# A trunk step with gathered experts on one core: expert sums assigned by the mixing item behind them, and layer 1's modulation made by PE alone

## What is computed

```python
def trunk_layer(x, cond, p, lambda_init, cache):
    sh1, sc1, g1, sh2, sc2, g2 = jnp.split(jax.nn.silu(cond) @ p['w_mod'] + p['b_mod'], 6, axis=-1)
    mix, ctx_tensors = token_mixing(modulate(x, sh1, sc1), p, lambda_init, cache)
    x = layer_norm_affine(DEEPNORM_ALPHA * x + g1[:, None] * mix, p['ln1_g'], p['ln1_b'])
    ffn = peer_ffn(modulate(x, sh2, sc2), p['peer_w_q'], p['peer_subkeys'], p['peer_u'], p['peer_v'])
    x = layer_norm_affine(DEEPNORM_ALPHA * x + g2[:, None] * ffn, p['ln2_g'], p['ln2_b'])
...
    def expert_block(args):
        xt, e, g = args
        act = jax.nn.gelu(jnp.einsum('td,tkd->tk', xt, jnp.take(u_tab, e, axis=0)), approximate=False) * g
        return jnp.einsum('tk,tkd->td', act, jnp.take(v_tab, e, axis=0))
```

## Time and the profile before

| | before |
|---|---|
| time, median of 3 runs | 3299.2 us (3292.91 to 3309.16) |
| time of the profiled execution | 3296.41 us |
| its span | 3294.6 us |
| mean granted TensorE clock | 0.888 |
| bytes moved | 1071.02 MB, mean 325 GB/s |

### The profile page before, as it was taken

The page is one execution under the profiler, slowest core; times in us unless marked ns, Lnnn a source line. Parts: engine busy times, 40 slices in busy tenths (PEclk is TensorE's granted clock), DMA queues, the critical chain, the costliest instruction groups (busy, mean ns, idle before and its releaser), DMA issues.

```text
span 3294.6 us, 29983 instructions
## 1 busy us (share of the span) xinstructions
PE 2524.8 (77%) x8820; PEld 1448.2 (44%) x8820; DVE 2202.0 (67%) x5396; ACT 710.8 (22%) x1797; POOL 1713.7 (52%) x1540
## 2 busy tenths in 40 slices
PE   8897988989767787668885779697958666667666
PEld 3585635757453223346652234475736322222222
DVE  4534577675769976756659744868665978856665
ACT  1121123451112220033211111254111211111111
POOL 0000275453437775445557744554433688777775
PEclk9898998989889998889997989898979898799988
DMA  8856598878778999979999978887966899999998
GB/s 327 299 187 222 175 377 311 295 268 324 276 262 334 376 396 414 364 292 374 408 412 343 359 274 302 330 325 271 352 231 240 308 339 342 357 378 415 416 412 313
DMA packets 296223, 1071.02 MB, mean 325 GB/s; under 512 B 33536, under 2 KB 36352, under 8 KB 295296
## 3 DMA queue, kind: packets, MB, share of 16 engines
q0 software_dynamic: 221184, 805.40, 64.9%
q1 hardware_dynamic: 71712, 253.16, 20.8%
q10 hardware_dynamic: 3168, 10.55, 0.8%
HBM read 1065.67 MB, written 3.31 MB: 324 GB/s over the span
## 4 chain that ended last, share of the span: by engine, by line
PE 42%; DVE 22%; POOL 16%; issue 10%; DMA 8%; ACT 1%; DVEq 0%; ACTq 0%; SPq 0%; POOLq 0%
POOL ring L1669 10%; PE psum L707 9%; PE psum L797 9%; POOL work L1669 6%; PE psum L786 5%; PE psum L956 5%; DVE ring L1221 4%; DMA ring<-in_peer_v,experts 3%; DVE work L1319 3%; PE psum L822 3%; PE psum L938 2%; PE psum L748 2%; DMA wring<-in_wpack 2%; DMA ring<-in_peer_u,experts 2%; DVE work L1221 2%
## 5 line engine op out<-in xcount | busy, mean ns | idle before, releaser
L707 PE MATMUL psum<-ring,wdiag 128*128 128x512 f32 x1680 | 915.7, 686 | 383.3 <-DMA ring<-in_peer_v,experts 210.2
L1669 POOL DMA_INDIRECT ring<-in_peer_u,experts x488 | 562.4, 1153 | 989.3 <-DVE dots L1221 455.8
L1669 POOL DMA_INDIRECT ring<-in_peer_v,experts x620 | 675.0, 1089 | 404.3 <-PE psum L707 210.8
L707 PEld LDWEIGHTS psum<-ring,wdiag 128*128 128x128 f32 x1680 | 341.3, 216 | 888.2 <-issue 537.5
L1221 DVE CUSTOM_DVE_ANT_0 work<-work 128x1024 f32<-128x1024 f32 x280 | 338.5, 1225 | 129.5 <-DMA work<-in_peer_u,experts 127.8
L1669 POOL DMA_INDIRECT work<-in_peer_u,experts x280 | 313.9, 1121 | 96.6 <-issue 83.2
L1221 DVE CUSTOM_DVE_ANT_0 ring<-ring,h2a 128x1024 f32<-128x1024 f32 x256 | 305.1, 1222 | 73.2 <-DMA ring<-in_peer_u,experts 72.3
L1221 DVE CUSTOM_DVE_ANT_0 ring<-ring,work 128x1024 f32<-128x1024 f32 x232 | 280.1, 1223 | 101.2 <-DMA ring<-in_peer_u,experts 99.8
L990 ACT ACTIVATE acts<-dots 128x2 f32<-128x2 f32 x384 | 77.8, 203 | 1104.1 <-DVE dots L1221 1056.7
L797 PE MATMUL psum<-work,wring 128*128 128x256 f32 (+1 forms) x1696 | 311.6, 342 | 0.6 <-DVE work L1630 0.6
L797 PEld LDWEIGHTS psum<-work,wring 128*128 128x128 f32 x1696 | 275.6, 195 | 43.4 <-issue 15.4
(11 more groups left out here) (201 smaller groups left out, 2872.7 us busy)
## 6 DMA issues: line engine op xcount, KB each, us to landing
wring<-in_wpack SPq DMA_DIRECT2D x374, 512.0 KB, 6.9
ring<-in_wpack SPq DMA_DIRECT2D x94, 512.0 KB, 5.6
ring<-in_peer_v,experts POOLq DMA_INDIRECT x620, 6.4
ring<-in_peer_u,experts POOLq DMA_INDIRECT x488, 6.4
work<-in_peer_u,experts POOLq DMA_INDIRECT x280, 6.3
work<-in_rows ACTq DMA_DIRECT2D x4, 1024.0 KB, 8.4
work<-in_peer_v,experts POOLq DMA_INDIRECT x148, 6.3
work<-in_rpb ACTq DMA_DIRECT2D x2, 1024.0 KB, 13.1
```

The costliest lines, as they stand in the source:

```text
L707: last = nc.tensor.matmul(psum[:, 6 + q, :], wdiag[:, SUM_NO[e] % SMALL, :], row(V_SLOT[e])[:, 512 * q:512 * (q + 1)], start=(e % KSEL == ...
L1669: pool.indirect_dma_start(row(slot), None, a[table], index).then_inc(got[slot], 16)
```

## The change

Three things are edited.

- `SHARE` goes. For each expert, `vector_sums()` looks up the item of `WORK` that stands behind the step of its sum, and takes a fraction for VectorE by the item's kind: in latent stages from `LATENT_SHARE`, in context stages 1/4, and none where the item is `topk`, `norms` or `ln1`. The first eight experts of a tile go to PE. Where no item is left, the fraction is 1/4. VectorE's sums by tile: 53, 18, 39, 84, 18, 30 before, and 53, 14, 9, 63, 9, 30 now, 178 instead of 242.
- In layer 1 all twelve modulation parts are `mod` items, on PE; parts 4 to 9 were `macc` items. Layer 0 stays as it is.
- ScalarE evacuates layer 1's parts and their `modt` (parts 0 to 9 were VectorE's).

The cost table is unchanged, but a `mod` item counts 7 where two `macc` counted 12, so the steps are dealt a little differently over layer 1's context stage: 13 steps instead of 16 stand between its first projection and its norms.

```diff
-SHARE = [[(44, 2, 3), (112, 1, 2)], [(72, 1, 3)], [(8, 1, 2), (72, 1, 8)], [(8, 3, 4), (104, 1, 2)], [(56, 1, 4)], [(8, 1, 4)]]
-def by_vector(e):
-    k = e % KSEL
-    part = [(n, of) for first, n, of in SHARE[e // KSEL] if k >= first]
-    return bool(part) and (k + 1) * part[-1][0] // part[-1][1] > k * part[-1][0] // part[-1][1]
...
 def mod_by_vector(l, j):
-    return 4 <= j < (12 if l == 0 else 10)
+    return l == 0 and j >= 4
...
             out += ([modt(l, 3 + j)] if j else [])
+            if j < 6:
+                out += [("macc", m, 4 + j, k, l) for k in range(2)] if mod_by_vector(l, 4 + j) else [("mod", m, 4 + j, l)]
...
+LATENT_SHARE = {"proj": (1, 1), "mix": (1, 1), "pq": (1, 1), "gate": (2, 3), "br": (2, 3), "ps": (1, 1), "h2": (1, 1),
+                "s": (1, 3), "pt": (1, 3), "o": (1, 3), "ot": (1, 3), "tt": (1, 3), "kv": (1, 3), "mqt": (1, 3), "mkt": (1, 3)}
+def vector_sums():
+    at, out = schedule(), []
+    for e in range(ALL_EXPERTS):
+        k, place = e % KSEL, at[e // PAIR + LAG_SUM]
+        x = WORK[place] if place < len(WORK) else ("end", -1)
+        n, of = LATENT_SHARE.get(x[0], (0, 1)) if x[1] in LATENT else (0, 1) if x[0] in ("topk", "norms", "ln1") else (1, 4)
+        out.append(2 * LAG_SUM <= k and (k + 1) * n // of > k * n // of)
+    return out
...
     if kind in ("mod", "modt"):
-        return "v" if x[2] < 10 or mod_by_vector(x[3], x[2]) else "a"
+        return "a" if x[3] else "v"
...
-                    elif kind == "mod" and it[2] >= 10:
+                    elif kind == "mod" and EVAC_BY[INDEX[it]] == "a":
                         full(act, it)
-                        if it[3]:
-                            full(act, modt(it[3], 9))
+                        if it[2] > 1:
+                            full(act, modt(it[3], it[2] - 2))
+                        else:
+                            act.wait_ge(experts_ready, HEAD_GROUPS * TILE_NO[(l, 0)])
+                            act.wait_ge(cols_ready, DEPTH)
                         taken(nc.scalar.copy(v.modacc[0:2, it[2] % 2, :], bank(it)[0:2, :]))
```

More of the change, by code:

```diff
@@ L318, in schedule @@
             at[n] = last
-    assert at == sorted(at) and all(s[0][0] >= 2 * LAG_SUM for s in SHARE)
+    assert at == sorted(at)
     return at
@@ L341, with by_vector, sums_before @@
 PROGRAM = program()
+LATENT_SHARE = {"proj": (1, 1), "mix": (1, 1), "pq": (1, 1), "gate": (2, 3), "br": (2, 3), "ps": (1, 1), "h2": (1, 1),
[8 more added lines that the diff above has]
+    return out
+VECTOR_SUM = vector_sums()
+def by_vector(e):
+    return VECTOR_SUM[e]
+SUM_NO, _sums = [], {True: 0, False: 0}
+for _e in range(ALL_EXPERTS):
+    SUM_NO.append(_sums[by_vector(_e)])
+    _sums[by_vector(_e)] += 1
+def sums_before(e, vector):
+    return sum(by_vector(i) == vector for i in range(e))
 XN_NO, _made = {}, 0
@@ L756, in _ @@
                         else:
[L757 removed]
+                            pe.wait_ge(macc_ready, j - 3)
                         for n in range(4):
@@ L1496, in _ @@
                             normalised(m, i, i)
-                    elif kind == "mod" and it[2] < 10:
+                    elif kind == "mod" and EVAC_BY[INDEX[it]] == "v":
                         full(dve, it)
@@ L1500, in _ @@
                             full(dve, modt(it[3], it[2] - 2))
-                        elif it[3]:
-                            full(dve, modt(0, 11))
                         taken(nc.vector.tensor_copy(v.modacc[0:2, it[2] % 2, :], bank(it)[0:2, :]))
```

11 lines of the change are left out of this document (2 added, 9 removed).

## The result

The changed kernel takes 3207.22 us (median of 4 runs, 3187.23 to 3213.1) against 3296.05 us before in the same comparison: a ratio of 0.970, 95% interval 0.9663 to 0.9738, that is 86 to 111 us less (the medians lie 89 apart, the ratio over all runs gives 99). The forecast was 3266 with a range down to 3232: the direction was right, the size not.

What follows compares the result with a forecast made beforehand. No single engine was taken to bound the kernel, so stretches were priced separately: -12 +15 -10 -10 -16 = -33 from 3296.4, plus 2.8 to the median, gave 3266 us; range for 8 in 10: 3232 to 3304.

Steps and rivals of the forecast that it cites:

- A: Layer 1's modulation loop: without the VectorE link 140 us against 168, -28; three steps displaced elsewhere +16; net -12 us.
- the third rival: Faster by more: displaced steps fill the norms gap and POOL issues faster beside less VectorE work; 3238 us, chance 0.14.
- The limit of about 358 GB/s a core: HBM to SBUF limit: the new loop could not be under 161 us, making its term +9; 3 in 100.
- B: Rest of layer 1's context stage: 19 more sums on PE up to the first top-k piece, net +15 us.
- C: Context-stage top-k: 13 VectorE sums go, eight where VectorE is the bound, the others worth 0; -10 us.
- The heads of layer 1: Latent stage of layer 1: 14 more head sums on PE, 9 priced at 1.72 us, +15; bounds -6 and +24.
- The rival with 38 paid sums: Slower, PE becomes the bound: every PE sum added in heads and context stage is paid, +65; total 3313 us, chance 0.14.
- Layer 0's +8.6: Attention heads of layer 0's latent stage: 5 more sums on PE, costing 8.6 us.
- the queries with `ln1`: Latent stages: 7 fewer PE sums at the queries, -12 each layer; fewer VectorE sums in `ln1`, -5 and -6 us.
- the top-k starts' direction: Start of the latent top-k: 4 fewer VectorE sums in each layer, -5 us each.
- the norms of layer 1: Layer 1's latent stage: 4 fewer VectorE sums in the norms, partly on its chain, -3 us.
- Tile 4's -3: Nine fewer VectorE sums in tile 4, where POOL's gather issues are the chain; -3 us.

Runs made afterwards that it cites:

- the modulation alone: The changed kernel with the old table of sums (242 on VectorE), so only layer 1's modulation moves to PE: 3256.16 us, 0.9863 of the kernel before.
- the sums alone: The changed kernel with layer 1's parts 4 to 9 and their evacuations back on VectorE, so only sums move: 3238.29 us, 0.9794 of the kernel before.
- `relief`: The kernel before without 19 VectorE expert sums in layer 1's heads, which nobody makes: 3368.79 us, 0.9973 of the kernel before on the same chip.
- `evac_vector`: The changed kernel with layer 1's modulation parts evacuated by VectorE instead of ScalarE: 3298.4 us, 0.9748 of the kernel before on the same chip.
- `warm_loop`: The kernel before with eight zero products on PE before the weight wait in layer 1's later projections: 3391.46 us, 1.0002 of the kernel before.
- the fraction 0: The changed kernel with no VectorE sums beside attention-head items (fraction 0 for 1/3, 21 fewer): 3227.05 us, 0.976 of the kernel before.

## Why the prediction fell short

**A, the modulation loop: the link was right, the size and what follows from it were not.** The new loop "has no VectorE link", and PE's round was forecast at 19 us and takes 19.51. But I set the loop's length by the transfers, at 140 us. It took 125.5 in that cut, and its window of 131 us moved 131 * 0.414 = 54 MB, not 57.5: I had counted the bytes of a stretch of 168 us, of which a shorter one holds fewer gathers that merely pass by. The loop is bound by PE and by transfers at once (125.74 of 131 us busy, DMA share 1.03). It gave 43 instead of 28. The three displaced steps were to cost 16 elsewhere: they are worth 18.5 in the loop and putting them back changes no total, so as a price that term stands. Net of them the loop gives 25 where 12 stood. But the modulation alone gave 40, so the net -12 was short by 28, and some 15 of them are neither in the loop nor in the steps. The likely place is the norms gap. I had left it to the third rival; before, it moved 172 GB/s, and with the change 413 (34 and 32 us, so 5.8 and 13.2 MB). The modulation alone fills it as well, the sums alone do not:

```profile
1367.00:1401.00 34.00, 26.03 (x125) 16.41 (x123) 19.39 (x51) 11.00 (x30) 12.06 (x11) 0.90 1.03 413
```

```profile
1401.00:1435.00 34.00, 26.78 (x137) 18.06 (x135) 18.93 (x53) 10.10 (x24) 3.31 (x4) 0.90 0.54 191
```

7.4 MB more in a gap that got no longer are 18 us of transfers at 413 GB/s (an estimate), in a stage whose rest is full of transfers. That is the first half of the third rival's mechanism. The gap is filled with the 16 steps put back too (393 GB/s), so it goes with the faster loop and not with the displaced steps; that it is worth the 15 us is argued, since no run isolates it and the scatter is of that size. The limit of about 358 GB/s a core in the Trainium skill's "DMA: Bandwidth & Descriptors", section "Where 436 GB/s comes from", to which I gave 3 in 100, fell: 414 GB/s over these 131 us. The Trainium skill's section gets it by halving a stack's 716 GB/s between two cores, and here one core ran the kernel alone.

**B and C, the rest of the context stage.** "7 * 1.72 = +12" for the sums on PE's chain, +15 with the others: -0.2 in the change, and the sums alone cost 3.7 us there. Too large, likely by the same error as the heads. On the two other chips it is 5.7 and 8.2 us (from the last projection to the key scores 305.2 in `relief` against 310.9 in `evac_vector`, 305.5 in `warm_loop` against 313.7 in the change), so a part of the price is real. C: I let 8 of 13 VectorE sums count and called the other five hidden; the stretch gave 14.7 with the sums alone, 1.13 us for each of the 13, within a scatter of some us. In the change it gave 14.0 where C and the +16 of the steps made +6.

**The heads of layer 1, the term whose mechanism was wrong: +15, measured +0.8** (261.7 to 262.5 us up to the first output product; the row's -2.7 has the output products in it). By size it comes second, 14 us, behind the 28 of A's net. The step was "Where PE has the chain each costs 1.72; where VectorE has it nothing". Two things were missing. The price: 0.86 us, since PE was 88% busy and the granted clock rises from 0.89 to 0.95 with more work. And the other side: where VectorE has the chain, taking a sum from it gains, 0.74 measured, and I had written zero there, a cost without its credit. The two near-equal numbers make the whole move nearly free, up to the point where the fraction 0 shows the price again (+8 us). The rival with 38 paid sums fell by the same numbers. Layer 0's +8.6 is not shown wrong: its first output product begins at 816.9 us in the mean of the eight kernels with the new sums, 810.7 in that of the five with the old ones.

**Right:** the queries with `ln1` (-17 forecast, -13.2 measured; -18, -20.1 in layer 1), the top-k starts' direction (-5 forecast in layer 1, -7.9 measured), the evacuations at nothing, the last tile bound by its transfers, and POOL as what is late next in the top-k.

**Wrong in sign:** the norms of layer 1 (-3 forecast, +4.3 measured), and the lead-in to the loop, +7.1 in the change but -1.4 to +4 in its variants, so mostly scatter, of the start and of the clock. Tile 4's -3, and the contention of GpSimd with two-input VectorE instructions (the Trainium skill's "GPSIMD Engine Reference", section "Key points") behind the third rival, found no support in these runs: 0.99 us an issue without a VectorE sum in tile 5 and 1.17 in tile 4, inside what stands with them.

**Open:** why tiles 4 and 5 of the change took 17.5 us more in its profiled execution. On this chip the same gathers take 0.97 to 1.03 us to issue in tile 5 from run to run, and nothing that was varied moved it. What the filled norms gap is worth. And how the 12.4 us that holding the slots leaves of the link part into VectorE's time and the clock.

## What to carry to other kernels

When work moves from one engine to another in a stretch where the chain alternates between the two, price both sides at every place, the credit as well as the debit; here they nearly cancelled (0.86 and 0.74 us), until PE was 94% busy. A PE that is granted less than the full clock can have more room than its busy share says: here a third of the added work came back by the clock. And a link through a slower engine that holds weight slots costs its own time and the refill behind it: for the length without it, take the new round of the engine that remains, and scale the bytes of gathers with the new length, not with the old, and look behind the loop for a place with idle transfers: what the shorter loop no longer moves may move there for nothing.

## What the runs showed of the hardware

The same kernel takes 2.6 to 2.9% longer on other chips: before took 3296 to 3300 us in three comparisons, 3381.89 and 3391.49 on two other chips. The change was worth less on the one where it ran again, 2.3% instead of 3.0%, and with VectorE's evacuation 2.5% on the other. The last tile of the change on such a chip:

```profile
2950.00:3250.00 300.00, 195.21 (x327) 72.12 (x326) 165.69 (x294) 35.68 (x136) 216.70 (x208) 0.82 0.96 365
```

208 gathers in 300 us where the other showed 225, 365 GB/s instead of 393, and 216.70 / 208 = 1.04 us an issue. The granted clock is lower there too, but what is short is gathers: the loop and the heads keep their length (120.7 us from the first to the last product of layer 1's projections, 123.5 on the other; 262.7 and 262.5 us for layer 1's heads). Totals are compared here only as ratios to a kernel on the same chip for that reason.

Within one chip, 19 added PE sums of 1.72 us at the full clock cost 0.86 each and raised the granted clock of their stretch from 0.89 to 0.95 (0.98 where PE was 94% busy). In layer 1's projections, which waited for another engine, 31 us more of busy PE were free altogether (1.0002).
